# Six weight loads of a decoder step, each issued as three DMAs over partitions 0-7, 8-15 and 16-127

## The reference

```python
hdn = jax.nn.silu(xf @ w1) * (xf @ w3)
acc = acc + ge[:, None] * (hdn @ w2)
```

## Time and profile before

| | us |
|---|---|
| median of 3 runs (713.18 to 718.21) | 717.13 |
| the profiled execution, device time | 715.49 |
| its span, first to last instruction | 713.7 |

### The profile page before, as it was taken

How to read it: one execution, slowest core, us unless ns; L and a number is a source line. 1 busy time by engine, 2 the same in 40 slices (tenths; PEclk the granted TensorE clock), 3 DMA queues, 4 the chain that set the end, 5 groups by cost and what they waited for, 6 DMA issues and landing times.

```text
span 713.7 us, 13633 instructions
## 1 busy us (share of the span) xinstructions
PE 594.4 (83%) x6073; PEld 366.3 (51%) x6073; DVE 221.8 (31%) x537; ACT 84.0 (12%) x225; POOL 54.0 (8%) x58
## 2 busy tenths in 40 slices
PE   7999899999999999999677687766778768777783
PEld 6878687775473555545343344333444334443341
DVE  4159996982141362222111111111111111111113
ACT  2311233320001330000000000000000000000012
POOL 4117421122000000000000000000000000000000
PEclk9999999999999999999889879898889887889897
DMA  9976989997999779999999999999999999999992
GB/s 301 292 295 231 345 159 424 375 364 301 407 414 412 306 268 420 419 424 427 424 423 424 423 428 425 424 423 423 426 426 423 426 421 426 423 422 423 420 368 82
DMA packets 42402, 269.15 MB, mean 377 GB/s; under 512 B 9844, under 2 KB 10672, under 8 KB 23903
## 3 DMA queue, kind: packets, MB, share of 16 engines
q1 hardware_dynamic: 29984, 229.34, 79.9%
q0 software_dynamic: 3072, 35.19, 12.0%
q10 hardware_dynamic: 9287, 3.74, 1.9%
HBM read 266.02 MB, written 2.46 MB: 376 GB/s over the span
## 4 chain that ended last, share of the span: by engine, by line
DMA 63%; PE 20%; issue 7%; DVE 6%; POOL 2%; ACT 1%; SPq 0%; POOLq 0%; DVEq 0%; ACTq 0%
DMA ring<-w_up 50%; DMA x<-w_up 6%; PE bank L1669 4%; PE bank L1650 3%; DVE ring L1057 3%; DMA ring<-cache_v,ridx 2%; PE bank L1404 2%; DMA ring<-cache_k,ridx 2%; DMA front<-q_scratch 1%; PE bank L1581 1%; PE bank L1604 1%; PE bank L1495 1%; PE bank L1500 1%; DMA q_scratch<-x 1%; DMA x<-x_prompt 1%
## 5 line engine op out<-in xcount | busy, mean ns | idle before, releaser
L1404 PE MATMUL bank<-ring,front 128*32 128x256 f32 x1856 | 157.4, 476 | 88.1 <-DMA ring<-w_up 75.6
L1404 PEld LDWEIGHTS bank<-ring,front 128*32 128x32 f32 x1856 | 85.1, 136 | 145.4 <-issue 121.6
L1266 DVE COPY front<-bank 128x256 f32<-128x256 f32 x32 | 13.6, 425 | 231.8 <-PE bank L1404 231.8
L1604 PE MATMUL bank<-hT,ring 128*128 128x264 f32 x256 | 59.8, 389 | 2.4 <-DMA ring<-w_in 1.9
L1420 PE MATMUL bank<-ring,front 128*32 128x256 f32 x928 | 55.4, 379 | 0.0
L1604 PEld LDWEIGHTS bank<-hT,ring 128*128 128x128 f32 x256 | 47.7, 190 | 12.0 <-DMA ring<-w_in 2.3
L1388 PE MATMUL bank<-front 128*32 128x256 f32 (+1 forms) x768 | 52.3, 385 | 0.3 <-DVE front L1169 0.3
L880 ACT ACTIVATE front<-bank 128x128 f32<-128x128 f32 x32 | 8.9, 278 | 369.6 <-PE bank L1412 369.6
L1509 PE MATMUL bank<-hT,ring 128*128 128x264 f32 x192 | 46.2, 399 | 0.0
L1276 DVE COPY front<-bank 128x256 f32<-128x256 f32 x32 | 13.6, 425 | 87.9 <-PE bank L1420 87.9
L1420 PEld LDWEIGHTS bank<-ring,front 128*32 128x32 f32 x928 | 29.9, 110 | 20.7 <-issue 1.1
(11 more groups left out here) (325 smaller groups left out, 559.9 us busy)
## 6 DMA issues: line engine op xcount, KB each, us to landing
ring<-w_gate SPq DMA_DIRECT2D x28, 2048.0 KB, 14.9
ring<-w_up SPq DMA_DIRECT2D x28, 2048.0 KB, 14.9
ring<-w_down SPq DMA_DIRECT2D x28, 2048.0 KB, 14.7
ring<-w_in SPq DMA_DIRECT2D x8, 2048.0 KB, 24.1
x<-w_gate SPq DMA_DIRECT2D x3, 2048.0 KB, 14.7
x<-w_up SPq DMA_DIRECT2D x3, 2048.0 KB, 14.7
x<-w_down SPq DMA_DIRECT2D x3, 2048.0 KB, 14.9
ring<-w_out SPq DMA_DIRECT2D x2, 2048.0 KB, 19.7
```

Source lines behind the costliest of these rows:

```text
L1266: v.tensor_copy(gu.rearrange("p (c n) -> p c n", c=2), bank[GATEUP][:, 0:QUART].rearrange("p (n c) -> p c n", c=2)).then_inc(s_gusb, 1)
L1404: last = m.matmul(bank[GATEUP][32 * g:32 * g + 32, 0:256], xgT[:, k % 2, k // 2], w[:, k, 256 * (g % 2):256 * (g % 2) + 256], start=k == 0 ...
L1604: last = m.matmul(out[:, 0:TOK], w[:, k, cols], hT[:, k, 0:TOK], start=k == 0, stop=k == DK - 1)
```

## The change

Gate and up of experts 27, 28 and 29 (`TILTED`, six loads) are issued as three DMAs in place of one: partitions 0 to 7, 8 to 15, and 16 to 127. The same bytes go to the same places. Each of the three adds 16 to the slot's semaphore, so such a load counts 48, and the tables of counts are built to fit. No other load, no wait and no computation is changed.

```diff
         home = {item: FREED[n % NSLOT] for n, item in enumerate(ORDER)}
-        arrived = {item: SLOT_BASE[home[item]] + 16 * (n // NSLOT + 1) for n, item in enumerate(ORDER)}
+        TILTED = [(e, m) for e in range(LAST - 4, LAST - 1) for m in range(2)]
+        arrived, slot_total = {}, list(SLOT_BASE)
+        for item in ORDER:
+            if item[0] < LAST:
+                slot_total[home[item]] += 48 if item in TILTED else 16
+                arrived[item] = slot_total[home[item]]
         later_home = [home[0, m] for m in range(3)]
-        later_base = [SLOT_BASE[q] + 16 * sum(home[item] == q for item in ORDER if item[0] < LAST) for q in later_home]
+        later_base = [slot_total[q] for q in later_home]
...
-        def load_matrix(eng, e, m, q):
+        def load_matrix(eng, e, m, q, tilted=False):
...
             if m < 2:
-                eng.dma_start(slot[q], src.rearrange("e (p k) f -> p (e k f)", p=P)).then_inc(s_slot[q], 16)
+                rows = src.rearrange("e (p k) f -> p (e k f)", p=P)
+                for part in (slice(0, NS), slice(NS, 2 * NS), slice(2 * NS, P)) if tilted else (slice(0, P),):
+                    eng.dma_start(slot[q][part], rows[part]).then_inc(s_slot[q], 16)
...
                 if e < LAST:
-                    load_matrix(sp, e, m, q)
+                    load_matrix(sp, e, m, q, (e, m) in TILTED)
```

## The result

The changed kernel takes 763.04 us (median of four runs, 761.98 to 765.35) where before, in the same comparison, takes 717.67: a ratio of 1.0635, with an interval of 1.059 to 1.068. It is slower by about 45 us. The forecast was 737.0 with a range of 714 to 749: right about the side, outside its range in size. The profiled execution after took 761.98 us, its span is 760.2 us.

A forecast was written before the change was run, and what follows sets the result against it. The prediction took the stream of DMA loads up to the landing of (30,1) as the bound. 715.5 us profiled + 0 for issues + 20.6 for slower split loads gave 736.1, plus 1.6 to the median 737.7, stated as 737; range 714 to 749.

The forecast's parts named there:

- What bounds the kernel: DMA, 63% of the chain: loads one after another until (30,1) lands at 679.41 us, whose shift moves the end one for one.
- Twelve more DMAs at nothing: On SP's queue, two more issues per split load take 0.7 us, hidden by the stream; 0 us taken, 4 us without cover.
- (a): Rival, the forecast: split loads slow through clashes of engines writing to the same part of SBUF; 724 to 749 us, chance 0.72.
- The signs: From 614.0 us on: issues 7 to 11 us apart, share near 1, 230 to 330 GB/s, PE's waits 5 to 10 us longer per expert.
- The price of a tilted load: On the half with 9 partitions: 9 x 0.615 x 1.67 = 9.2 us, 4.3 over 4.92; six loads 25.9 us.
- two thirds of that surcharge: Discount on the extra time per split load: factor 1.67, where the full surcharge gives 11.1 us a load.
- nearest row: The state_pool load, to 120 of 128 partitions: one KB of stream lost for one moved, 11.1 us per tilted load.
- The head start of 5.3 us: At the end, eight engines finish 5.3 us before the others; taken off the 25.9 us, leaving 20.6.
- The levelling: Six loads give the early half of the engines 3.7 us more and the other 3.7 less; (30,1) would land 1.6 us earlier.
- (b): Rival: the split costs nothing beyond its bytes and the early half gets them; -1.6 us, 715.5 us, chance 0.18.
- (c): Rival: the split costs nothing beyond its bytes, but the extra goes to the late half; +3.7 us, 720.8 us, chance 0.07.
- (d): Rival: engines share out pieces differently from 9 and 7, so nothing is levelled; no change, 717 us, chance 0.03.

The follow-up runs named there:

- cols3: Changed kernel, but the six loads are cut by columns into three DMAs over all 128 partitions; 716.66 us, ratio 1.0014 to the kernel before.
- apart_gates: Changed kernel, but only the three gate loads of experts 27 to 29 are cut, at partition 64; 750.62 us, ratio 1.0498 to the kernel before.
- one_load: Changed kernel, but only load (27,0) is split into partitions 0-7, 8-15 and 16-127; 727.37 us, ratio 1.0122 to the kernel before.
- p16_112: Changed kernel, but the six loads go as two DMAs, partitions 0-15 and 16-127; 760.38 us, ratio 1.0622 to the kernel before.
- p64_64: Changed kernel, but the six loads go as two DMAs, partitions 0-63 and 64-127; 758.51 us, ratio 1.0596 to the kernel before.
- wide_tilt: Changed kernel, but the six loads go as five DMAs of rows 16, 16, 8, 4 and 2 apart; 741.12 us, ratio 1.033 to the kernel before.
- home_tilt: Changed kernel, but only the gate loads are split: odd rows, every fourth from 2, four 8-row pieces; 726.56 us, ratio 1.0139 to the kernel before.
- meet_no: Changed kernel, six loads: half the columns whole, the rest as four 8-row DMAs, rows four apart, partitions 32-127 left out; 708.98 us, 0.9898 of before.
- meet_yes: Same as meet_no, but each 8-row DMA takes neighbouring partitions (0-7, 8-15, 16-23, 24-31); 719.02 us, ratio 1.0044 to the kernel before.
- tail_spread: Changed kernel, six loads: seven eighths of the columns whole, the last eighth as 16 DMAs of 8 rows four apart; 738.28 us, 1.0318 of before.

## Why the prediction was wrong in size

**What bounds the kernel: right.** The end moved with the landing of (30,1): it came 46.2 us later, of which 44.7 us lie behind the issue of (27,0), and the tail of 34.6 us is as it was. DMA's part of the chain rose from 63% to 66%.

**Twelve more DMAs at nothing: right.** cols3 shows it, with 1.0014.

**The mechanism of (a): right in what it said of the engines' packets.** The share stays at 1, the packets get longer, the rate falls, and the number of DMAs has no effect. That they clash at the receiving side isn't shown. The signs were set too mild: the rate was to be 230 to 330 GB/s and was 218 to 251, and PE's waits were to grow by 5 to 10 us and grew by 11.8 (6.26 to 18.1).

**The price of a tilted load: wrong, and this is the step that failed.** The text took "two thirds of that surcharge", a factor of 1.67, for six loads. Two things were off in it. The factor is 2: SP's ten steps lie between 6.6 and 12.0 us, the middle ones at 9.8, twice 4.92, and packets of 16 KB took 1201 ns where they took 617. A factor of 2 was the prediction's own nearest row. And it holds for nine loads, not six: the packets of the whole down loads took 615 ns where they took 314. The reason given for the discount was that "part of the loss is suffered by the regular stream next to it, and here a third of the traffic in the stretch is regular". The first half of that sentence is true and should have raised the sum, since the down loads are part of the same stream and every load waits for the one three places before it. The stretch that the prediction priced shows it as well: from 220 to 229 us before, beside norm_final, 207 regular packets of 16 KB took 650 ns each, where they took 613 from 216 to 219.5 us. apart_gates and one_load show it directly, since a cut load costs 11.7 and 9.9 us where its own doubling is 4.9. With the factor 2 and nine loads the term is 9 x 4.92 = 44.3 us, beside 44.0 measured. This sum was made after the result; its two factors rest on the packets' times.

**The head start of 5.3 us: wrong to take it off.** The term was worked out for the half with 9 rows and reduced by the lead of that half. But p16_112, with 8 rows for every engine, loses as much as the change, so the loss doesn't need the extra rows of one half, and it isn't paid for out of that half's lead. The levelling itself did take place: the plateau of the earlier trace rows went away, and after a share of 0.91 there is 0.35 in the next microsecond and 0.22 in the one after, while p64_64, whose engines all get 8 rows, keeps a share of 0.50 to 0.54 from 735 to 739 us. No gain from it can be seen. (30,1) takes 16.2 us from issue to landing instead of 15.54, and the change's ratio is 1.0635 beside 1.0622 for p16_112. The intervals of these ratios are some 3 us to either side, more than the 1.6 us that the levelling was to give.

**The rivals.** (b), (c) and (d) were given 0.28 together. The tilt without the loss, on which (b) and (c) rest, couldn't be tried by itself: wide_tilt and home_tilt, the nearest to it, brought the loss with them in part. meet_no, in which eight engines also get more than the others, is 6.7 us faster, which is about what its missing bytes alone were expected to give, and tells nothing for (b). The upper end of the range, 749, was the full surcharge, but for six loads and less the head start. It left out the whole loads beside the split ones and took off a lead that doesn't count, so the truth lay outside it.

## What to carry to other kernels

In a stream like this one, a load over 128 partitions should stay whole, or be cut by columns or by strides of 2 or 4; a cut at partition 64 or 16 halved the rate here. When a stream slows because one of its members is awkward, price it by the time that the awkward one is in flight, with all loads that are in flight beside it, and not by its own bytes. And a DMA share of 1 says that engines are occupied, not how fast they move bytes: read GB/s beside it.

## What the runs showed of the hardware that was not expected

- The same 64 + 64 rows cost 43 us as 0-63 and 64-127, and nothing as even and odd. The Trainium skill's page "DMA: Bandwidth & Descriptors", section "Rules for kernel authors", says of two transfers to disjoint partition halves: "Don't bother — they serialize". The runs show more: done in that way the stream ran at 218 GB/s, the whole loads beside the halves were slowed too, and the ratio was 1.0596, while with alternate partitions there was no loss.
- One split load of 2 MB slows the stream for some 20 us (228 GB/s between two stretches above 410) and costs 9.9 us. Packets of whole loads beside it take 585 ns in place of 314.
- Spacing alone is no cure: loads with 16-row pieces of rows 8 apart still cost, at 269 GB/s, and those with 32-row pieces of rows 4 apart don't, at 424.
- What an issue costs SP depends on the DMA's rows. Four DMAs of 8 rows took 2.7 us in meet_no (rows four apart) and 1.3 us in meet_yes (neighbouring rows), 0.67 and 0.33 us each. With 64 rows the spacing made no difference: both halves together took 1.1 us in p64_64 and in even_odd. Up to six pieces (3.9 us in home_tilt) the issues stay below the 4.92 us of a load, and sixteen (10.8 us in tail_spread) don't.
